# Bias tables built between the adaLN units of the prologue, and stored ahead of x

## The reference

```python
cs = jax.nn.silu(c)
for layer in range(DEPTH):
    mod = (cs @ P['ada_w'][layer] + P['ada_b'][layer]).reshape(N, 6, 1, D_MODEL)
    h = _rmsnorm(x, P['norm_mix_g'][layer]) * (1 + mod[:, 1]) + mod[:, 0]
    ...mixer, gated residual...
    h = _rmsnorm(x, P['norm_ffn_g'][layer]) * (1 + mod[:, 4]) + mod[:, 3]
    gu = h @ P['ffn_w_gate_up'][layer]
    x = x + mod[:, 5] * ((jax.nn.silu(gu[..., :FFN_HIDDEN]) * gu[..., FFN_HIDDEN:]) @ P['ffn_w_down'][layer])

def _group_bias(rel_bias_table, grp, dist):
    tab = rel_bias_table[:, grp * B_HPG:(grp + 1) * B_HPG]
    return jnp.moveaxis(tab[_t5_bucket(dist)], -1, 0).astype(jnp.float32)

s = jnp.einsum('znqhd,znkhd->znhqk', qb, kk).astype(jnp.float32) * (Dh ** -0.5) + bias[None, None]
```

## Time and profile before

| | us |
|---|---|
| median of 3 executions | 2721.53 |
| lowest, highest | 2717.16, 2722.25 |
| the profiled execution | 2721.19 |
| its span, first to last instruction | 2719.4 |

### The profile page before, as it was taken

One profiled execution on the slowest core, in us unless ns is written; L12 is line 12 of the kernel. 1 busy time (PEld: TensorE's weight loads), 2 busy tenths in 40 slices (PEclk: granted clock), 3 DMA queues, 4 the chain that ended last, 5 costly groups with the idle time before them and its releaser, 6 DMA issues.

```text
span 2719.4 us, 35656 instructions
## 1 busy us (share of the span) xinstructions
PE 2533.0 (93%) x16005; PEld 2411.7 (89%) x16005; DVE 961.0 (35%) x1556; ACT 571.4 (21%) x722; POOL 528.9 (19%) x175
## 2 busy tenths in 40 slices
PE   7798889688899999999999799997999999999996
PEld 4797778457899999999999799997999999999996
DVE  3465653346422222122224522436422222222226
ACT  3312223422411111111112311032311111111112
POOL 1321001100322211222112423111422211122220
PEclk8899999788999999999999899999999999999998
DMA  8112242563112221122212388310011111111101
GB/s 308 58 59 88 86 130 87 199 207 105 47 63 78 78 93 63 63 94 78 77 64 77 118 284 289 112 56 32 32 47 47 47 47 39 40 47 47 47 32 64
DMA packets 163522, 246.66 MB, mean 91 GB/s; under 512 B 5870, under 2 KB 150676, under 8 KB 162218
## 3 DMA queue, kind: packets, MB, share of 16 engines
q1 hardware_dynamic: 151078, 179.41, 20.1%
q0 software_dynamic: 3872, 60.82, 6.5%
q10 hardware_dynamic: 8420, 4.15, 0.5%
HBM read 225.69 MB, written 62.52 MB: 106 GB/s over the span
## 4 chain that ended last, share of the span: by engine, by line
PE 74%; DVE 3%; DMA 2%; issue 1%; ACT 1%; SPq 0%; DVEq 0%; ACTq 0%
PE ps L1845 67%; PE ps L1882 2%; PE ps L1956 1%; PE ps L1900 1%; DVE nt L1345 1%; DMA scratch_o<-o_rows 1%; DMA cache<-in_cache_b_kv 1%; DMA w_raw<-in_e_w_out 0%; PE ps L2097 0%; DVE h_lo L1371 0%; DVE nt L1354 0%; DVE tmp L1196 0%; PE ps L2086 0%; PE ps L1964 0%; DVE ln_t L1475 0%
## 5 line engine op out<-in xcount | busy, mean ns | idle before, releaser
L1688 POOL TENSOR_TENSOR w_lo<-w_raw,w_hi 128x2048 fp32r<-128x2048 f32 x93 | 435.5, 4683 | 1789.0 <-ACT w_hi L911 1789.0
L1845 PE MATMUL ps<-h_hi,w_hi 128*128 128x352 f32 x3024 | 667.8, 329 | 6.1 <-DVE h_lo L1213 3.4
L1845 PE MATMUL ps<-h_hi,w_lo 128*128 128x352 f32 x3024 | 653.6, 324 | 0.0
L1845 PE MATMUL ps<-h_lo,w_hi 128*128 128x352 f32 x3024 | 653.4, 324 | 0.0
L1845 PEld LDWEIGHTS ps<-h_hi,w_hi 128*128 128x128 f32 x3024 | 511.7, 190 | 27.0 <-issue 22.4
L1845 PEld LDWEIGHTS ps<-h_hi,w_lo 128*128 128x128 f32 x3024 | 520.7, 188 | 0.0
L1845 PEld LDWEIGHTS ps<-h_lo,w_hi 128*128 128x128 f32 x3024 | 516.2, 189 | 0.0
L1206 DVE SCALAR_TENSOR_TENSOR x<-ps,mod,x 128x704 f32<-128x704 f32 x448 | 315.5, 746 | 317.0 <-PE ps L1845 317.0
L1253 DVE TENSOR_TENSOR tmp<-ps,tmp 128x1056 f32<-128x1056 f32 x44 | 55.3, 1257 | 729.7 <-PE ps L1845 729.7
L911 ACT ACTIVATE w_hi<-w_raw 128x2048 fp32r<-128x2048 f32 x93 | 177.7, 1911 | 503.9 <-PE ps L1845 400.4
L1845 PE MATMUL ps<-mid_hi,w_hi 128*128 128x352 f32 x1248 | 274.6, 328 | 8.5 <-DVE acc_s L1207 5.2
(11 more groups left out here) (260 smaller groups left out, 1705.0 us busy)
## 6 DMA issues: line engine op xcount, KB each, us to landing
w_raw<-in_ada_w SPq DMA_DIRECT2D x48, 1024.0 KB, 6.6
w_raw<-in_ffn_w_gate_up SPq DMA_DIRECT2D x44, 1024.0 KB, 5.1
out_kv_sample<-in_cache_b_kv POOLq DMA_DIRECT2D x8, 4088.0 KB, 19.3
w_raw<-in_ffn_w_down SPq DMA_DIRECT2D x22, 1024.0 KB, 5.0
cache<-in_cache_b_kv SPq DMA_DIRECT2D x28, 512.0 KB, 6.2
w_raw<-in_e_w_in SPq DMA_DIRECT2D x11, 1024.0 KB, 5.7
w_raw<-in_o_w_in SPq DMA_DIRECT2D x10, 1024.0 KB, 10.2
out_kv_sample<-in_cache_b_kv POOLq DMA_DIRECT2D x8, 1016.0 KB, 6.4
```

Source lines behind the costliest of these rows:

```text
L1688: pool.tensor_tensor(w_lo[raw_of[u].slot], w_raw[raw_of[u].slot], w_hi[u % 2].bitcast(F32), ALU.subtract)\
L1845: mm = pe.matmul(big(t)[:, b, 0:BLK], wt, xt[:, k, b * BLK:b * BLK + BLK], start=(k == 0 and n == 0), stop=(k == K - 1 and n == 2))
```

## The change

The single item `rel` is cut into 14 items `rel_step`, one for each table. Seven stand between the first adaLN unit and the first tile of x, and one between each later adaLN unit and its tile of x. Each takes the next number of the small PSUM tiles. The item `rel` that is left holds no work of TensorE or VectorE; in it GpSimd now stores `rel_rep` and `bias_s0` first, then splits the first weight tile, and then stores x.

```diff
--- before.py
+++ after.py
@@ -146,8 +146,7 @@
     vec: int = 0
     c: int = 0
     ext: int = 0
-    rel: int = 0
-    rels: int = 0
+    steps: list = None
     x: int = 0
     v: int = 0
     new: int = 0
@@ -246,11 +245,21 @@
         return out
 
     items.append(Item("setup", vec=take("misc"), c=take("misc"), ext=take("misc")))
+    rels = [Item("rel_step", n=n) for n in range(14)]
+
+    def rel_step():
+
+        step = rels[sum(1 for it in items if it.kind == "rel_step")]
+        step.misc = take("misc")
+        items.append(step)
+
     for k in range(KT):
         ada()
+        for _ in range(7 if k == 0 else 1):
+            rel_step()
         items.append(Item("x_in", k=k, x=take("big")))
     ada_out()
-    items.append(Item("rel", rel=take("misc", 12), rels=take("misc", 2)))
+    items.append(Item("rel", steps=[it.misc for it in rels]))
 
     def norm(layer, which):
         items.append(Item("norm", layer=layer, which=which, n=take("norm"), big=take("big")))
@@ -1294,14 +1303,13 @@
                         dve.tensor_copy(x[:, it.k, SEQ:TOK], big(it.x)[:, 2, 0:S_TOK]).then_inc(big_free[it.x % 2], 1)
                     if it.k:
                         add_square(0, it.k - 1)
-                elif it.kind == "rel":
-                    for n in range(12):
-                        q = it.rel + n
-                        dve.wait_ge(misc_ready, q + 1)
+                elif it.kind == "rel_step":
+                    n, q = it.n, it.misc
+                    dve.wait_ge(misc_ready, q + 1)
+                    if n < 12:
                         dve.tensor_copy(rel_rep[:, n, 0:REL], misc(q)[:, 0:REL]).then_inc(left(q), 1)
-                    for n in range(2):
-                        q = it.rels + n
-                        dve.wait_ge(misc_ready, q + 1)
+                    else:
+                        n -= 12
                         for s in range(3 * n, min(3 * n + 3, NS)):
                             own(dve.scalar_tensor_tensor(bias_s0[:, 0, :], misc(q)[:, 160 * (s % 3):160 * (s % 3) + 160],
                                                          row_step[:, s:s + 1], mask_s[:, 0, :] if s == 0 else bias_s0[:, 0, :],
@@ -1719,17 +1727,17 @@
                     pool.dma_start(st_rows, A["state_a_conv"][0].rearrange("(h b) t c -> (b t) h c", h=2))\
                         .then_inc(tabs_loaded, 16)
                 elif it.kind == "rel":
+                    misc_evacuated(pool, it.steps[11])
+                    misc_evacuated(pool, it.steps[10])
+                    pool.dma_start(d_rel.rearrange("g (p n) -> p g n", n=384)[:, :, 0:REL], rel_rep[:, :, 0:REL])\
+                        .then_inc(rel_stored, 16)
+                    misc_evacuated(pool, it.steps[13])
+                    misc_evacuated(pool, it.steps[12])
+                    pool.dma_start(d_bias, bias_s0.rearrange("p g n -> p (g n)")).then_inc(rel_stored, 16)
                     split_lo(0)
                     for t in x_tiles:
                         big_evacuated(pool, t)
                     pool.dma_start(d_x, x.rearrange("p k n -> p (k n)")).then_inc(x_stored, 16)
-                    misc_evacuated(pool, it.rel + 11)
-                    misc_evacuated(pool, it.rel + 10)
-                    pool.dma_start(d_rel.rearrange("g (p n) -> p g n", n=384)[:, :, 0:REL], rel_rep[:, :, 0:REL])\
-                        .then_inc(rel_stored, 16)
-                    misc_evacuated(pool, it.rels + 1)
-                    misc_evacuated(pool, it.rels)
-                    pool.dma_start(d_bias, bias_s0.rearrange("p g n -> p (g n)")).then_inc(rel_stored, 16)
                 elif it.kind == "norm":
                     n, c = it.n, 6 * it.layer + 3 * it.which
                     if n == 0:
@@ -1929,16 +1937,16 @@
                         pe.transpose(big(t)[:, n // 4, (n % 4) * P:(n % 4) * P + P], x_tok[:, n, k * P:k * P + P], ident)
                     pe.transpose(big(t)[:, 2, 0:S_TOK], xs_tok[:, k * P:k * P + P], ident[0:S_TOK, 0:S_TOK])\
                         .then_inc(big_ready, 1)
-                elif it.kind == "rel":
-                    pe.wait_ge(tab_made, 1)
-                    for n in range(12):
-                        q = it.rel + n
-                        misc_slot(q)
+                elif it.kind == "rel_step":
+                    n, q = it.n, it.misc
+                    if n == 0:
+                        pe.wait_ge(tab_made, 1)
+                    misc_slot(q)
+                    if n < 12:
                         pe.matmul(misc(q)[:, 0:REL], tab_b[:, n, :], oh_p[:, n // HPG, :], start=True, stop=True)\
                             .then_inc(misc_ready, 1)
-                    for n in range(2):
-                        q = it.rels + n
-                        misc_slot(q)
+                    else:
+                        n -= 12
                         for s in range(3):
                             mm = pe.matmul(misc(q)[:, 160 * s:160 * s + 160],
                                            tab_s[:, max(0, 3 * n + s - 3)].rearrange("k h t -> k (h t)"),
```

## The result

| | before | after |
|---|---|---|
| median (lowest to highest), us | 2719.49 (2716.91 to 2722.25) | 2725.28 (2722.05 to 2728.29) |
| executions | 13 | 13 |
| the profiled execution / its span | 2721.19 / 2719.4 | 2722.41 / 2720.6 |

The ratio is 1.0024, with a 95% interval of 1.0016 to 1.0031: slower by 5.8 us. The forecast was 2725.2.

A forecast was written before the change was run, and what follows sets the result against it. The prediction took TensorE (74% of the chain) as the bound, with the first projection's start deciding. Its terms, -17.8 + 0.6 + 9.9 + 10.9 + 0.3 = +3.9 (forward +4.0), on 2721.19 gave 2725.2 us, range 2716 to 2730.

The forecast's parts named there:

- Removed: Block of table steps between the last tile of x and the mean: its removal saves 17.8 us if nothing is added.
- Seven steps ahead of x: Prologue, TensorE's wait for x: seven steps of 1.27 us mostly fit there, delaying x by 0.6 us.
- Steps in the units: Loop over x on TensorE, without gaps: five table steps of 1.27 and two sample steps of 1.78 add 9.9 us.
- The clock: Loop over x: TensorE stays at 1.2 GHz throughout instead of rising to 2.4 near 35, adding 10.9 us; chance 0.57.
- Waits for the PSUM tile: Units of the loop: table steps wait for VectorE to free a reused tile, +0.3 us; at most 3 x 1.0 at high clock.
- Sum: Whole prologue: all terms add to +3.9 us, or +4.0 counted forward to the mean.
- Stores: Table stores and store of x on GpSimd: the earlier table stores take away no wait and stay covered, worth 0.
- rival D: First normed tile: table stores still land last, gate the norm and lose the gain; given no chance of its own.
- Rivals A: Loop over x: the clock is high from the first tile, -14.1 us, 2707 us; chance 0.05.
- rival B: Loop over x: the clock rises mid-loop as before, -10.4 us, 2711 us; breaks even for a rise at 62; chance 0.11.
- Rival C: First projection: loop low as forecast, then more time at half clock; slower than 0.2%, 2727 to 2730 us; chance 0.27.

The follow-up runs named there:

- e3: The changed kernel with the 12 prompt table steps padded with zeros from 33 to 128 rows; 2711.51 us, ratio 0.9974 to the kernel before.
- e5: The changed kernel with each interleaved table step behind its tile of x instead of ahead of it; 2725.73 us, ratio 1.0030 to the kernel before.
- e11: The changed kernel once more, unedited, one execution; 2723.44 us.
- e10: The kernel before once more, unedited, one execution; 2713.52 us.
- e4: The kernel before with the 12 prompt table steps padded with zeros from 33 to 128 rows; 2717.48 us, ratio 1.0001 to the kernel before.
- e2: The changed kernel with seven table steps ahead of x and the other seven in one block behind all units; 2715.54 us, ratio 0.9988 to the kernel before.
- e1: The changed kernel with GpSimd's old order (split, store of x, then table stores); 2741.06 us, ratio 1.0087 to the kernel before.
- e8: The changed kernel with 128-row prompt steps, 12 steps ahead of x, 2 behind the units, GpSimd's split first; 2704.98 us, ratio 0.9953 to the kernel before.
- e7: The changed kernel with 128-row prompt steps, nine steps ahead of x, five behind the units, GpSimd's split first; 2702.69 us, ratio 0.9949 to the kernel before.
- e6: e2 with GpSimd's split of the first weight tile ahead of the table stores; 2708.45 us, ratio 0.9970 to the kernel before.
- e9: e8 with the split behind the table stores and held until VectorE's sums of squares are done; 2708.59 us, ratio 0.9966 to the kernel before.

## Why the prediction was right, and where it was not

The outcome and its mechanism came as forecast: the clock stays at 1.2 GHz through the whole loop, and this eats the 17.8 us that the removed block gives. By its own steps:

- **Removed, -17.8.** Between the end of ScalarE's square and VectorE's sum the prediction put 0.03 us, with no row for it; it is 75.65 - 75.00 = 0.65, so -17.2. In e3 the same place takes 0.23, and why it differs stays open.
- **Seven steps ahead of x, +0.6.** They run from 14.94, 1.27 apart, and x starts 0.8 later: +0.8. The cover held.
- **Steps in the units, +9.9.** This is the term that was most mis-sized. A unit grew from 4.96 to 6.53, so a step costs 1.57 and not 1.27, and one with a sample step lasts 6.85, so that costs 1.89 and not 1.78: 5 x 1.57 + 2 x 1.89 = 11.6. The 1.27 had been read in a row of equal steps, where the weight load starts 0.42 us ahead of its own matmul, beside the one before (17.23 and 17.65); in the unit both start at 29.13, so the load isn't hidden.
- **The clock, +10.9**, as forecast, and e5 and e11 repeat the low clock. The size hangs on the execution of the kernel before that is taken: in e10 its loop took 47.38 - 23.27 = 24.1 us, which makes the term 12.8. Of its two reasons one held. That 33 rows count for little: e3 and e4 confirm it from both sides, with the number of rows the only thing edited in TensorE's work. That the step parts the product from the transposes: e5 puts them together and nothing changes, so this reason fell. What is left, that the step thins the other work out, fits e2 (no step in the loop, clock up at 31.9) and e5, but is inferred from them: narrow steps were only tried at one per unit.
- **Waits for the PSUM tile, +0.3.** TensorE starts the step right as VectorE frees the tile, and the units with such a wait are no longer than the others: nothing measurable. The 1.0 that it named for the high clock is what e3 shows (1.09).
- **Sum.** -17.2 + 0.8 + 11.6 + 10.9 = 6.1, beside 6.34 at the mean and 5.8 between the medians. The forecast had 4.0. That it met the median within 0.1 us is luck: it started from the one profiled execution, 2721.19, which stands 1.7 above the median of 13. Started from that median it would have been 2723.5.
- **Stores, 0.** True against the kernel before (the bias store, issued at 71.91, took 4.6 us, and its reader came at 85.39), but for a reason that the prediction didn't state. It said that the earlier stores take no wait away; e1 shows that with the old order the new schedule would have waited 15.5 us. The prediction weighed only the whole change and so missed that half of the change pays for what the other half would cost. Its rival D, dismissed with no chance, is what happens without the reordering.

Rivals A and B needed the clock to rise amid narrow steps. The Trainium skill ("TensorE: Matmul & The Clock Gate", "Part 1: The HAM clock gate") has it that sustained matmul activity releases the clock. The runs agree where the steps have 128 rows (up at 17.0 in e3, at 15.9 in e8) and disagree for 33 rows (48.7 us of a TensorE without a gap, and no rise). Rival C was not needed for the sign: the prologue alone is 6.3 us slower. By the ratio the change does end above the 0.2% at which C began, through the mis-sized steps and not through C's cause, a clock that is worse in the first projection; that took 1.5 us off the lag in one pair of profiles and added 1.5 in the other. The prediction also held that a difference under 5.4 us can hardly be told from none; with 13 executions each the interval of 1.0016 to 1.0031 is well clear of none. And by its own figures rival B breaks even for a rise at 58.3, not 62 (24.0 + 11.6, and 10.4 / 0.457 later); nothing else hangs on that.

A saving of 17 us was there to be had. In the change two things took it, 11.6 us of TensorE time in a loop without gaps and 10.9 of clock. Where half of the steps were kept out of the loop (e2), the clock came back, and a split on GpSimd held VectorE for 4.5.

## What to carry to other kernels

Moved work is free only in the piece that fits into idle time: here seven narrow steps in the wait for x cost 0.8 us (and nine wide ones nothing: in e7 TensorE still waited 1.15 us for x behind them), while one narrow step in each unit of a gapless loop cost its full length plus the clock of the loop. Before few-row matmuls are put into a loop that lives near the change of clock, fill their rows with zeros or keep them out. When a block goes, ask what it covered: here a store of x, a table store, and a split on GpSimd that must not meet VectorE's critical sum. And once the clock is up, look for the next limit: in e8 it was the adaLN loads, 3.0 us a unit.

## What the hardware showed unexpectedly

- A VectorE addition of two operands in on-chip memory, 1.23 us alone, took 5.70, 5.00 and 2.71 us when it met GpSimd's 4.5 us split, each time ending about 1.1 us after the split (63.48, 56.09, 56.13); moved apart in e6 and e9 it took 1.23. This looks like exclusion and not sharing, and it goes both ways: in e5 the split, which met a sum already under way, took 5.11 us instead of 4.50, and the next VectorE operation then waited for its end. VectorE's copies out of PSUM in the kernel before took their 0.56 us beside the same split. The Trainium skill ("SBUF — State Buffer", "SBUF: two separate sides") describes such a lock between GpSimd and a VectorE operation with two operands in on-chip memory, held for a whole instruction by whichever starts first. The runs agree, but for the order in e2, where by the trace VectorE started 0.10 us before the split (58.88 and 58.98) and was held all the same.
- The zeros cost TensorE nothing and gave a higher clock: the seven table steps ahead of x took 6.33 us with 128 rows and 9.30 with 33.
